# A bank split moved from token 334 to token 332, and GpSimd's low parts written as two operations

## The chip, the cores and the metric

The kernel runs on one core of a Trainium2 chip. The metric is the device time of one execution in microseconds (us); of several runs the median is shown. TensorE is called PE here (its matmuls PE, its weight loads PEld), VectorE DVE, ScalarE ACT, GpSimd POOL, and the DMA-issuing SyncE SP.

## The reference

One step of a small streaming encoder with two layers, on 528 prompt tokens (16 of them learned) and 8 sequences of 16 tokens that continue from carried state. All of it is float32.

```python
def trunk(x, ...):
    for i in range(DEPTH):                      # DEPTH = 2
        h = rmsnorm(x, norm_mix[i])
        if i % 2 == 0: m, s = gla_mixer(h, ...)         # gated linear attention
        else:          m, s = shortconv_mixer(h, ...)
        x = x + m
        f, s = conv_ffn(rmsnorm(x, norm_ffn[i]), ...)
        x = x + f
    return rmsnorm(x, norm_final), ...

def shortconv_mixer(h, buf, w_in, conv_w, w_out):
    bg, cg, u = jnp.split(h @ w_in, 3, axis=-1)
    y, new_buf = causal_dwconv(cg * u, buf, conv_w)     # depthwise, width 3, over tokens
    return (bg * y) @ w_out, new_buf

def conv_ffn(h, buf, w_up, conv_w, conv_b, w_down):     # 1024 -> 2 * 2816 -> 1024
    z = h @ w_up
    zc, new_buf = causal_dwconv(z, buf, conv_w)
    gate, up = jnp.split(zc + conv_b, 2, axis=-1)
    return (jax.nn.silu(gate) * up) @ w_down, new_buf
```

## The kernel before

The activations lie as x[128, 8, 656]: 1024 features in 8 tiles of 128 partitions, and for each tile a row of 656 tokens (528 prompt tokens, then 128 sample tokens), 4 bytes each, so that token t of a tile stands at byte 4t of the tile's row.

**Products.** Each float32 product is made of three passes in a 4-byte matmul type (fp32r): a high part (xh, wh, gh) and a low part (xl, wl, gl), as wh with xh, wh with xl, and wl with xh. The weights come in 512 KB units [128, 8, 128] into a ring of four. For every unit SP loads `raw`, ACT casts the high part `wh` (function `high`, line 1244), POOL subtracts to get the low part `wl` (function `low`, line 355; a few units are done by DVE at line 807), and only then may PE use the unit. A core's PSUM is used as four slots of two banks. A product's token range doesn't fit one bank of 512, so every pass is a **pair** of matmuls, one per bank, cut at a token that `banks(first, cut)` gives.

**Token ranges.** The products don't need the earliest tokens of the later stages, so a stage begins at token `first` and ends at 656: 0 in the attention's input projections, 8 in its output projection, 8 and 12 in the up projections of the ffn of layers 0 and 1 (`FIRST_Z`), 12 in the short convolution mixer (`FIRST_MIX`) and in the down projection of layer 0, 16 in the down projection of layer 1. The cut is `middle(first)`, half way, except in the up projections, where it is half way through the prompt part (`middle(first, PROMPT)`), so that DVE can take the prompt part of both banks in one operation.

**Stages.** PE's stream of work: attention projections (`project`, line 409, one unit = 8 feature tiles x 3 passes = 24 pairs), attention (to about 330 us), its output projection, then per layer the ffn in 11 groups: four up units (`z`), then `project_down` (line 425: 8 output tiles m, each two weight tiles x 3 passes = 6 pairs), with the mixer of layer 1 between the two ffns. The groups of an ffn run in a loop written for all engines. The order of work on each engine is written out by hand. For every output tile m of a down projection DVE adds the product to x (`add_to_x`, line 801) and with it frees the PSUM slot; PE waits for the slot (`open_slot`) four steps later. A `z` unit is taken by DVE in `take_padded` (lines 1032 to 1040) which frees its slot, then convolved (`convolve`, lines 1009 and 1013, three operations), and every second one gated (`gate_hidden`, lines 1020 to 1026). DVE reaches the adds of a down projection only behind the take and the convolution of the group's last `z` unit. The sum of squares for a norm is added by DVE at line 770 and summed over partitions by PE at line 437.

Of the kernel before, what the change touches and what calls it, by code (L numbers as in the profile page):

```python
# [21 lines left out]
F32 = mybir.dt.float32  # L22
# [141 lines left out]
def build(nc, x_in, w_in, wgd_in, wgu_in, par_in, reset_in, mask_in, s0_in, zc_in,  # L164
# [126 lines left out]

    def banks(first, cut):

        return (0, first, cut), (BANK, cut, TOK)
# [19 lines left out]
    def from_token(first, ap, p):  # L314

        return two(ap[:, first:TOK]), slot(p, (TOK - first) // 2)
# [27 lines left out]
    def _(pool):  # L344
# [8 lines left out]
        def low(j, done):  # L353
            pool.wait_ge(sem["hi_done"], done)
            pool.tensor_tensor(wl[:, j, :, :], raw[:, j, :, :], wh[:, j, :, :].bitcast(F32),  # L355
                               ALU.subtract).then_inc(sem["lo_done"], 1)
# [26 lines left out]
    def _(pe):  # L383
# [32 lines left out]
        def project_down(step, first, f0, n_ready, rings, i=0, release=1, g_count=None):  # L416
# [3 lines left out]
            for m in range(KT):  # L420
                p = open_slot(step(m), i)
                for f in range(2):
                    for w, v in ((wh, gh), (wh, gl), (wl, gh)):
                        for c, a, z in banks(first, middle(first)):
                            mm = pe.matmul(ps[:, p, c:c + z - a], w[:, rings[f], m, :], v[:, f0 + f, a:z],  # L425
                                           start=(f == 0 and w is wh and v is gh), stop=(f == 1 and w is wl))
                            if m == 0 and f == 0 and w is wh and v is gh and c:
                                mm.then_inc(sem["units_used"], release)
# [227 lines left out]
        for layer in range(2):  # L656
            if layer == 1:

                for g in range(MIX_G):
                    for j in range(6):  # L660
                        project(("mix", g, j), xh, xl, n_unit + 1, n_unit % RING, FIRST_MIX, middle(FIRST_MIX),
# [12 lines left out]
            def z_units(g, i=0, release=1, norm=None):  # L674
                nonlocal n_unit
                for j in range(4):
                    u = n_unit + j
                    project(("z", layer, g, j), xh, xl, 12 * i + (u + 1), u % RING, FIRST_Z[layer],
                            middle(FIRST_Z[layer], PROMPT), i=i,
# [68 lines left out]
    def _(dve):  # L748
# [49 lines left out]
        def add_to_x(p, m, first):  # L798

            tile, product = from_token(first, x[:, m, :], p)  # L800
            dve.tensor_tensor(tile, product, tile, ALU.add).then_inc(freed[p], 1)  # L801
# [241 lines left out]
        def z_unit(step, layer, z, j, i=0):  # L1043
# [5 lines left out]
            take_padded(p, j, rstd, FIRST_Z[layer], middle(FIRST_Z[layer], PROMPT))  # L1049
# [34 lines left out]
        def mixer():  # L1084
            dve.wait_ge(sem["zl_saved"], ZT)
            for g in range(MIX_G + 1):
                if g < MIX_G:
                    for e in range(2):
# [3 lines left out]
                        out, product = from_token(FIRST_MIX, bg[:, e, :], p)  # L1092
                        dve.tensor_tensor(out, product, two(rstd[:, FIRST_MIX:]), ALU.mult).then_inc(freed[p], 1)
                        p = take(("mix", g, 3 * e + 1))
                        out, product = from_token(FIRST_MIX, cg, p)
                        dve.tensor_tensor(out, product, two(rstd[:, FIRST_MIX:]), ALU.mult).then_inc(freed[p], 1)
# [6 lines left out]
                        take_padded(p, e, cg, FIRST_MIX, middle(FIRST_MIX))  # L1103
# [528 lines left out]
```

## Time and profile before

| | us |
|---|---|
| three runs | 1556.33, 1556.71, 1563.7 |
| median of them | 1556.71 |
| the profiled execution | 1557.0 |
| its span in the trace | 1555.2 |
| PE busy | 1532.7 (99%) |
| DVE busy | 1106.0 (71%) |
| POOL busy | 488.5 (31%) |
| ACT busy | 441.4 (28%) |

The time of an execution is its span plus 1.8 us around it. Matmuls overlap in the trace, so the mean time of one is longer than the pace at which they follow each other; the pace is read from the start times, or from the chain, where a run of matmuls stands with its length and its count. TensorE's granted clock was 2.4 GHz over all of the stretch from 330 to 1533 us.

### The profile page before, as it was taken

Reading aid. Unit: us, or ns where it says so; the run is one execution under the profiler, and the core shown is the slowest. Engines: PE = TensorE matmul, PEld = TensorE weight load, DVE = VectorE, ACT = ScalarE, POOL = GpSimd, SP = SyncE. Lnnn points to the kernel's source line nnn. Section 1 sums busy time; section 2 is a strip of 40 time slices with the busy share of each in tenths; the row PEclk is TensorE's granted clock in tenths of the full one; section 3 lists DMA queues with packets and bytes.
Section 4 is the critical chain, followed back from the end, with each engine's and each line's share of the span. In section 5 each row is a group of like instructions: output and inputs, shape, how many; then the busy total and the mean of one; then the engine's idle time right before and its main releaser. Section 6 shows DMA issues by size and latency. Waiting matters only on the chain.

```text
span 1555.2 us, 25977 instructions
## 1 busy us (share of the span) xinstructions
PE 1532.7 (99%) x10294; PEld 1514.5 (97%) x10294; DVE 1106.0 (71%) x1315; ACT 441.4 (28%) x692; POOL 488.5 (31%) x207
## 2 busy tenths in 40 slices
PE   7999999999999999999999999999999999999997
PEld 6999998899999999999999999999999999999996
DVE  6566665754977777777778645548977787777777
ACT  5355554343212121211215111115221212212123
POOL 2422221143233333323332333332333333233330
PEclk9999999999999999999999999999999999999998
DMA  6211116222222222122222222222222222222212
GB/s 216 80 55 55 55 55 239 90 72 69 68 76 74 68 81 79 57 80 71 78 71 65 92 82 68 82 68 78 66 78 72 77 81 66 68 81 67 77 47 78
DMA packets 34841, 123.76 MB, mean 80 GB/s; under 512 B 3888, under 2 KB 6832, under 8 KB 33616
## 3 DMA queue, kind: packets, MB, share of 16 engines
q1 hardware_dynamic: 31840, 108.37, 22.3%
q10 hardware_dynamic: 2928, 14.35, 2.5%
q8 instruction: 54, 0.88, 0.2%
q14 instruction: 19, 0.16, 0.0%
HBM read 114.48 MB, written 8.22 MB: 79 GB/s over the span
## 4 chain that ended last, share of the span: by engine, by line
PE 94%; DVE 3%; ACT 1%; DMA 1%; DVEq 1%; issue 0%; POOL 0%; SPq 0%; ACTq 0%
PE ps L409 64%; PE ps L425 21%; PE ps L611 2%; PE ps L511 2%; PE ps L710 1%; PE ps L635 1%; PE ps L563 1%; PE ps L525 0%; DVE sq L770 0%; DMA s<-states 0%; DMA raw<-w_units 0%; DVE x L1161 0%; PE ps L645 0%; DVE snew L979 0%; PE ps L492 0%; PE ps L437 0%
## 5 line engine op out<-in xcount | busy, mean ns | idle before, releaser
L355 POOL TENSOR_TENSOR wl<-raw,wh 128x1024 fp32r<-128x1024 f32 x190 | 472.3, 2492 | 966.9 <-ACT wh L1244 927.7
L409 PE MATMUL ps<-xh,wh 128*128 128x260 f32 (+3 forms) x2144 | 494.9, 312 | 0.0
L409 PE MATMUL ps<-xl,wh 128*128 128x260 f32 (+3 forms) x2144 | 493.5, 312 | 0.0
L409 PE MATMUL ps<-xh,wl 128*128 128x260 f32 (+3 forms) x2144 | 493.4, 312 | 0.0
L409 PEld LDWEIGHTS ps<-xl,wh 128*128 128x128 f32 x2144 | 382.5, 189 | 0.0
L409 PEld LDWEIGHTS ps<-xh,wh 128*128 128x128 f32 x2144 | 381.8, 189 | 0.7
L409 PEld LDWEIGHTS ps<-xh,wl 128*128 128x128 f32 x2144 | 382.2, 189 | 0.0
L1244 ACT ACTIVATE wh<-raw 128x1024 fp32r<-128x1024 f32 x196 | 204.2, 1055 | 302.1 <-PE ps L409 276.9
L801 DVE TENSOR_TENSOR x<-ps,x 128x644 f32<-128x644 f32 (+2 forms) x200 | 158.8, 823 | 94.7 <-PE ps L425 67.7
L1013 DVE SCALAR_TENSOR_TENSOR y<-zp,par,y 128x660 f32<-128x660 f32 (+1 forms) x192 | 185.7, 967 | 26.5 <-issue 21.7
L425 PE MATMUL ps<-gl,wh 128*128 128x322 f32 (+1 forms) x768 | 177.2, 312 | 0.0
L1389 ACT COPY zl<-zp 128x18 f32 (+1 forms) x88 | 18.3, 208 | 558.3 <-DVE y L1013 558.3
L425 PE MATMUL ps<-gh,wh 128*128 128x322 f32 (+1 forms) x768 | 175.9, 310 | 0.1
L425 PE MATMUL ps<-gh,wl 128*128 128x322 f32 (+1 forms) x768 | 175.2, 309 | 0.0
L425 PEld LDWEIGHTS ps<-gh,wh 128*128 128x128 f32 x768 | 129.7, 189 | 0.8 <-DVE x L801 0.7
L425 PEld LDWEIGHTS ps<-gh,wl 128*128 128x128 f32 x768 | 130.0, 189 | 0.0
L425 PEld LDWEIGHTS ps<-gl,wh 128*128 128x128 f32 x768 | 129.5, 189 | 0.0
L1009 DVE TENSOR_SCALAR y<-zp,par 128x660 f32<-128x660 f32 (+1 forms) x96 | 100.5, 1047 | 29.9 <-issue 27.0
L1032 DVE TENSOR_TENSOR zp<-ps,rstd 128x520 f32<-128x520 f32 (+1 forms) x88 | 61.1, 694 | 72.1 <-PE ps L409 68.7
L1026 DVE TENSOR_TENSOR gl<-hh,gh 128x644 fp32r<-128x644 f32 (+1 forms) x52 | 100.0, 1923 | 3.9
L1024 DVE CAST gh<-hh 128x644 fp32r<-128x644 f32 (+1 forms) x52 | 66.6, 1281 | 3.8
L1021 DVE TENSOR_TENSOR hh<-sg,y 128x128 f32<-128x128 f32 x44 | 52.2, 1187 | 0.0
(158 smaller groups left out, 1238.6 us busy)
## 6 DMA issues: line engine op xcount, KB each, us to landing
raw<-w_units SPq DMA_DIRECT2D x196, 512.0 KB, 3.5
s<-states ACTq DMA_DIRECT2D x4, 1024.0 KB, 6.0
state_sample<-snew ACTq DMA_DIRECT2D x4, 1024.0 KB, 4.1
x<-x_t SPq DMA_DIRECT2D x8, 328.0 KB, 8.3
x<-x_t ACTq DMA_DIRECT2D x1, 2624.0 KB, 13.1
y_t<-x SPq DMA_DIRECT2D x4, 384.0 KB, 2.4
y_t<-x SPq DMA_DIRECT2D x4, 256.0 KB, 2.2
ffn_last<-zl ACTq DMA_DIRECT2D x2, 396.0 KB, 3.4
```

What stands on the lines that cost most here:

```text
L355: pool.tensor_tensor(wl[:, j, :, :], raw[:, j, :, :], wh[:, j, :, :].bitcast(F32), ALU.subtract).then_inc(sem["lo_done"], 1)
L409: mm = pe.matmul(ps[:, p, c:c + z - a], w[:, ring, k, :], v[:, k, a:z], start=(k == 0 and w is wh and v is hi), stop=(k == KT - 1 and w is ...
L425: mm = pe.matmul(ps[:, p, c:c + z - a], w[:, rings[f], m, :], v[:, f0 + f, a:z], start=(f == 0 and w is wh and v is gh), stop=(f == 1 and ...
L511: return pe.matmul(queries(ps[:, p, :], a, z), ks[:, a:a + P], queries(qs, a, z), start=True, stop=True)
L801: dve.tensor_tensor(tile, product, tile, ALU.add).then_inc(freed[p], 1)
L1009: dve.tensor_scalar(out, src[:, first:YN], w_col(0), w_col(3) if bias else None, ALU.mult, ALU.add if bias else ALU.bypass)
L1013: last = dve.scalar_tensor_tensor(out=out, in0=src[:, first + j:YN + j], scalar=w_col(j), in1=out, op0=ALU.mult, op1=ALU.add)
L1021: dve.tensor_tensor(blocks(hh[:, PROMPT:TOK], SLEN), gate[1], blocks(up[:, SB:PADDED], SW)[:, :, 0:SLEN], ALU.mult)
L1024: dve.tensor_copy(gh[:, f, first:TOK], hh[:, first:TOK])
L1026: dve.tensor_tensor(gl[:, f, first:TOK], hh[:, first:TOK], gh[:, f, first:TOK].bitcast(F32), ALU.subtract).then_inc(sem["g_done"], 1)
L1032: dve.tensor_tensor(two(zp[:, zi, 2 + first:SB]), slot(p, cut - first), two(factor[:, first:PROMPT]), ALU.mult)
L1244: act.activation(wh[:, j, :, :], raw[:, j, :, :], ACT.Copy).then_inc(sem["hi_done"], 1)
```

## The change

`cut_of(first)` is `middle(first)` rounded down to a multiple of 4. It replaces `middle` in the down projections and the mixer's projections, and in the up projections of layer 1 it replaces the middle of the prompt part. Only ranges that begin at token 12 change: the mixer's and the down projection's pair goes from 322 and 322 tokens (cut at 334) to 320 and 324 (cut at 332), and layer 1's up pair from 258 and 386 (cut at 270) to 320 and 324. Ranges that begin at 0, 8 and 16 keep their cuts. `from_token` now gives a list, of one piece where both banks hold the same number of tokens, and of two where they don't: DVE's adds to x after a 12-token start, and its two takes per mixer tile, become two operations each; `take_padded` in layer 1 takes its other branch, three operations in place of two. And POOL's `low` becomes two operations over half of the feature tiles each, of which the second signals.

```diff
+    def cut_of(first):
+        return (first + (TOK - first) // 2) // 4 * 4
...
     def from_token(first, ap, p):
-        return two(ap[:, first:TOK]), slot(p, (TOK - first) // 2)
+        cut = cut_of(first)
+        if 2 * cut == first + TOK:
+            return [(two(ap[:, first:TOK]), slot(p, cut - first))]
+        return [(ap[:, a:z], ps[:, p, c:c + z - a]) for c, a, z in banks(first, cut)]
+
+    Z_CUT = (middle(FIRST_Z[0], PROMPT), cut_of(FIRST_Z[1]))
...
         def low(j, done):
             pool.wait_ge(sem["hi_done"], done)
-            pool.tensor_tensor(wl[:, j, :, :], raw[:, j, :, :], wh[:, j, :, :].bitcast(F32),
-                               ALU.subtract).then_inc(sem["lo_done"], 1)
+            for ks in (slice(0, KT // 2), slice(KT // 2, KT)):
+                last = pool.tensor_tensor(wl[:, j, ks, :], raw[:, j, ks, :], wh[:, j, ks, :].bitcast(F32),
+                                          ALU.subtract)
+            last.then_inc(sem["lo_done"], 1)
...
-                        for c, a, z in banks(first, middle(first)):
+                        for c, a, z in banks(first, cut_of(first)):
...
-                        project(("mix", g, j), xh, xl, n_unit + 1, n_unit % RING, FIRST_MIX, middle(FIRST_MIX),
+                        project(("mix", g, j), xh, xl, n_unit + 1, n_unit % RING, FIRST_MIX, cut_of(FIRST_MIX),
...
-                            middle(FIRST_Z[layer], PROMPT), i=i,
+                            Z_CUT[layer], i=i,
...
         def add_to_x(p, m, first):
-            tile, product = from_token(first, x[:, m, :], p)
-            dve.tensor_tensor(tile, product, tile, ALU.add).then_inc(freed[p], 1)
+            for tile, product in from_token(first, x[:, m, :], p):
+                last = dve.tensor_tensor(tile, product, tile, ALU.add)
+            last.then_inc(freed[p], 1)
...
-            take_padded(p, j, rstd, FIRST_Z[layer], middle(FIRST_Z[layer], PROMPT))
+            take_padded(p, j, rstd, FIRST_Z[layer], Z_CUT[layer])
```

The mixer's two takes (`bg`, `cg`) change in the same way as `add_to_x`, and its `take_padded` gets `cut_of(FIRST_MIX)`.

The instructions on PE at the start of layer 1's ffn, where the mixer's last down projection ends and the first up unit begins; before:

```order
L425 MATMUL ps<-gh,wh 128x322 x2
L425 MATMUL ps<-gl,wh 128x322 x2
L425 MATMUL ps<-gh,wl 128x322 x2
L409 MATMUL ps<-xh,wh 128x258
L409 MATMUL ps<-xh,wh 128x386
L409 MATMUL ps<-xl,wh 128x258
L409 MATMUL ps<-xl,wh 128x386
```

and in the changed program, at the same place:

```order
L436 MATMUL ps<-gh,wh 128x320
L436 MATMUL ps<-gh,wh 128x324
L436 MATMUL ps<-gl,wh 128x320
L436 MATMUL ps<-gl,wh 128x324
L436 MATMUL ps<-gh,wl 128x320
L436 MATMUL ps<-gh,wl 128x324
L420 MATMUL ps<-xh,wh 128x320
L420 MATMUL ps<-xh,wh 128x324
```

The number of matmuls and their order stay; a pair has 644 tokens before and now.

On DVE, in layer 1's ffn, a `z` unit is taken, convolved and gated; before:

```order
L1032 TENSOR_TENSOR zp<-ps,rstd 128x516
L1040 TENSOR_TENSOR zp<-ps,rstd 128x8x16
L1009 TENSOR_SCALAR y<-zp,par 128x656
L1013 SCALAR_TENSOR_TENSOR y<-zp,par,y 128x656 x2
L1020 TENSOR_TENSOR hh<-sg,y 128x512
```

and now:

```order
L1047 TENSOR_TENSOR zp<-ps,rstd 128x320
L1049 TENSOR_TENSOR zp<-ps,rstd 128x196
L1052 TENSOR_TENSOR zp<-ps,rstd 128x8x16
L1021 TENSOR_SCALAR y<-zp,par 128x656
L1025 SCALAR_TENSOR_TENSOR y<-zp,par,y 128x656 x2
L1032 TENSOR_TENSOR hh<-sg,y 128x512
```

One operation on the 516 prompt tokens has become two, ahead of the convolution; the rest is as before. In layer 0's down projections DVE's `x<-ps,x 128x644` has become `128x320` and `128x324` in the same way.

## Rows read from the trace of the kernel before

**Rows 1.** The page, part 1: busy times, share of the span, instructions.

```profile
PE 1532.7 (99%) x10294; PEld 1514.5 (97%) x10294; DVE 1106.0 (71%) x1315; ACT 441.4 (28%) x692; POOL 488.5 (31%) x207
```

**Rows 2.** Busy times by stretch (length, busy us and counts, granted clock).

```profile
330.00:1533.00 1203.00, 1202.87 (x8069) 1201.21 (x8068) 877.09 (x996) 276.04 (x472) 400.62 (x164) 1.00 0.24 73
```

**Rows 3.** Groups of PE's matmuls by form: count | busy us, mean ns | idle.

```profile
L409 PE MATMUL ps<-xh,wl 128*128 128x386 f32 x352 | 120.5, 342 | 0.0
...
L409 PE MATMUL ps<-xh,wl 128*128 128x388 f32 x352 | 119.6, 340 | 0.0
...
L425 PE MATMUL ps<-gh,wl 128*128 128x322 f32 x480 | 109.7, 310 | 0.0
...
L409 PE MATMUL ps<-xh,wl 128*128 128x322 f32 x384 | 88.1, 311 | 0.0
```

**Rows 4.** The chain in order of time: start us, us, what, matmuls.

```profile
441.29 28.53 PE ps L409 x192
...
555.57 14.31 PE ps L425 x96
...
943.24 42.81 PE ps L409 x288
...
1130.09 14.04 PE ps L425 x96
1144.13 28.60 PE ps L409 x192
1172.73 7.03 PE ps L425 x48
...
1258.30 14.07 PE ps L425 x96
```

**Rows 5.** PE's timeline, output projection: first and last of 44 rows (a row: one pair).

```profile
333.12 0.46 PE L409 MATMUL ps<-oh,wh 128*128 128x324 f32 x2
...
345.83 0.46 PE L409 MATMUL ps<-ol,wh 128*128 128x324 f32 x2
```

**Rows 6.** Timelines of DVE, POOL and PE around the first norm.

```profile
21.23 5.82 DVE L770 TENSOR_TENSOR sq<-sq 128x656 f32<-128x656 f32 x2
...
20.90 5.44 POOL L355 TENSOR_TENSOR wl<-raw,wh 128x1024 fp32r<-128x1024 f32 x2 [18.19 <-ACT wh L1244]
...
27.10 1.37 PE L437 MATMUL ps<-sq,ones 128*128 128x328 f32 x4 [0.98 <-DVE sq L770]
```

**Rows 7.** Timeline at 1172 us: DVE and POOL behind a group's last z unit.

```profile
1172.76 0.70 DVE L1032 TENSOR_TENSOR zp<-ps,rstd 128x516 f32<-128x516 f32 x1 [0.78 <-PE ps L409]
...
1173.38 0.28 DVE L1040 TENSOR_TENSOR zp<-ps,rstd 128x128 f32<-128x128 f32 x1
1174.05 2.81 DVE L1009 TENSOR_SCALAR y<-zp,par 128x656 f32<-128x656 f32 x1 [0.39 <-issue]
1174.10 2.40 POOL L355 TENSOR_TENSOR wl<-raw,wh 128x1024 fp32r<-128x1024 f32 x1 [6.76 <-ACT wh L1244]
...
1178.91 2.28 DVE L801 TENSOR_TENSOR x<-ps,x 128x640 f32<-128x640 f32 x3
```

**Rows 8.** DVE's timeline: the first add to x of two other groups.

```profile
561.51 0.82 DVE L801 TENSOR_TENSOR x<-ps,x 128x644 f32<-128x644 f32 x1
...
1264.21 0.82 DVE L801 TENSOR_TENSOR x<-ps,x 128x640 f32<-128x640 f32 x1
```

**Rows 9.** POOL's two subtractions: duration ns min/median/max.

```profile
L355 POOL TENSOR_TENSOR wl<-raw,wh x190: 2357/2409/4182, 20.9 to 1519.5; 128x1024 fp32r<-128x1024 f32 x190
...
L367 POOL TENSOR_TENSOR ol<-qk,oh x8: 1571/1604/2180, 277.6 to 325.2; 128x656 fp32r<-128x656 f32 x8
```

**Rows 10.** DVE's timeline in the mixer: a take in three operations.

```profile
864.37 0.49 DVE L1035 TENSOR_TENSOR zp<-ps,cg 128x322 f32<-128x322 f32 x1 [2.58 <-PE ps L409]
864.78 0.35 DVE L1037 TENSOR_TENSOR zp<-ps,cg 128x194 f32<-128x194 f32 x1
865.04 0.28 DVE L1040 TENSOR_TENSOR zp<-ps,cg 128x128 f32<-128x128 f32 x1
```

More of the change, by code:

```diff
@@ L1091, in mixer @@
                         p = take(("mix", g, 3 * e))
-                        out, product = from_token(FIRST_MIX, bg[:, e, :], p)
-                        dve.tensor_tensor(out, product, two(rstd[:, FIRST_MIX:]), ALU.mult).then_inc(freed[p], 1)
+                        for (out, product), (factor, _) in zip(from_token(FIRST_MIX, bg[:, e, :], p),
+                                                               from_token(FIRST_MIX, rstd, p)):
+                            last = dve.tensor_tensor(out, product, factor, ALU.mult)
+                        last.then_inc(freed[p], 1)
                         p = take(("mix", g, 3 * e + 1))
-                        out, product = from_token(FIRST_MIX, cg, p)
-                        dve.tensor_tensor(out, product, two(rstd[:, FIRST_MIX:]), ALU.mult).then_inc(freed[p], 1)
+                        for (out, product), (factor, _) in zip(from_token(FIRST_MIX, cg, p),
+                                                               from_token(FIRST_MIX, rstd, p)):
+                            last = dve.tensor_tensor(out, product, factor, ALU.mult)
+                        last.then_inc(freed[p], 1)
                         dve.drain()
@@ L1102, in mixer @@
                             dve.wait_ge(sem["cl_saved"], E - 1)
-                        take_padded(p, e, cg, FIRST_MIX, middle(FIRST_MIX))
+                        take_padded(p, e, cg, FIRST_MIX, cut_of(FIRST_MIX))
                         dve.drain()
```

## Prediction

> **What bounds the kernel now.** I read the page first: PE is busy 99% of the span, DVE 71%, POOL 31% [rows 1]. Since overlapping matmuls make "busy" a weak word, I read the busy times by stretch next: between 330 and 1533 us PE stands still for 0.13 of 1203 us, at a granted clock of 1.00, which is 2.4 GHz [rows 2]. So three quarters of the time is the pace at which PE's matmuls follow each other, and nothing else. An operation removed from DVE or POOL there is worth nothing unless PE was waiting for it; a faster pair of matmuls is worth all of its gain.
>
> Then I read that pace from the chain, as length over pairs (two matmuls make a pair) [rows 4]:
> - layer 1 down, 320 and 320 tokens: 14.04 / 48 = 292.5 ns
> - layer 0 down, 322 and 322: 14.31 / 48 = 298.1 ns
> - mixer, 322 and 322: 42.81 / 144 = 297.3 ns
> - layer 1 up, 258 and 386: 28.60 / 96 = 297.9 ns
> - layer 0 up, 260 and 388: 28.53 / 96 = 297.2 ns
>
> and for the output projection, 324 and 324, from the first and last start of 44 pairs: 12.71 / 43 = 295.6 ns [rows 5]. The reader is to see that 644 tokens cost as much as 648 or more, while 640 cost 5 ns less: layer 1's up pair has four tokens fewer than layer 0's and is 0.7 ns slower. By form the same shows: 386 columns have a mean of 342 ns, 388 columns 340 [rows 3]. What the slow pairs share is their cut: 334 or 270, not a multiple of 4. A token is 4 bytes, so I count groups of four tokens (16 bytes) that a piece touches. Cut at 334, both pieces touch the group 332 to 335: 81 + 81 = 162 groups for 161 groups' worth of tokens. At 270 it is 65 + 97 = 162. The aligned 648 is 162 too, and 640 is 160. The pace follows the groups.
>
> **The change, part by part.**
>
> *The cut at 332.* The new pair touches 80 + 81 = 161 groups. Its price is not in the trace. From halves: a 320 piece is 146.3 ns, a 324 piece is between 147.8 (rows 5) and 148.6 (half of layer 0's up pair, rows 4); together 294.1 to 294.9, and I take 294.5 [rows 4, 5]. How many pairs: a form's count stands for one of three passes and one of two equal pieces, so 386 columns make 352 x 3 = 1056 pairs, the mixer's 322 make 384 x 3 / 2 = 576, and the down projections' 322 make 480 x 3 / 2 = 720 [rows 3]. The sum:
> - up, layer 1: 1056 x (297.9 - 294.5) = 3.6 us
> - mixer: 576 x (297.3 - 294.5) = 1.6 us
> - down at 12 tokens: 720 x (298.1 - 294.5) = 2.6 us
>
> Together 7.8 us; at 294.9 it is 6.8, at 294.1 it is 8.7.
>
> What speaks against it is a rule: the Trainium skill, page "TensorE: Matmul & The Clock Gate", section "Back-to-back issue gap", gives a gap of N/2.4 + 2.5 ns for N columns, in which only the number of columns counts. By that rule a pair of 644 costs 273.3 ns before and after, and this part would save 0; the rows stand 25 ns above it and don't grow with N as it says between 644 and 648. The same skill, page "SBUF — State Buffer", section "Specifications (TRN2)", states 16-byte cachelines with a penalty for each new line; with that the rows agree.
>
> *DVE's extra operations.* An add to x or a take that was one operation becomes two: 120 adds (15 down projections of 8), 16 takes in the mixer, 44 in layer 1's up units, 180 in all. The price of one more: a take of 516 tokens holds DVE 0.62 us (1172.76 to 1173.38), while 322 and 194 tokens hold it 0.67 (864.37 to 865.04) [rows 7, 10]. That is 0.05 to 0.06 us each, 11 us of DVE in all. It lies beside PE's work: DVE is idle 29% of the time. It is on a path at one place per group, below.
>
> *POOL's two halves, first norm.* POOL's subtraction and a DVE operation with two inputs in SBUF shut each other out here: two adds of squares on 656 tokens take 5.82 us together while POOL does two subtractions from 20.90 on, where a 640-token add takes 0.82 [rows 6, 7]. Each waits out one whole POOL operation, and PE then stands still 0.98 us for the sum [rows 6]. Price of a half: POOL takes 2357 ns for 1024 elements and 1571 for 656, so 2.14 ns an element and 0.17 us fixed; 512 elements make 1.26 us [rows 9]. The two DVE adds then wait for one half each, about 1.2 us less each, and the sum is there 2 us earlier. PE's 0.98 us go. Nothing else held PE there, so the gain is 1.0 us.
>
> *POOL's two halves, in the groups.* Behind the last up unit of each group, DVE must take it, convolve it (three operations), and then make the first add to x, since PE's fifth output tile needs that slot. At 1172 us PE comes to the slot at 1172.73 + 7.03 = 1179.76 [rows 4] and the add ends at 1179.73 [rows 7], so no time is left over. In two other groups the add ends at 562.33 and 1265.03 [rows 8], where PE wants the slot at 555.57 + 14.31/2 = 562.73 and 1258.30 + 14.07/2 = 1265.34 [rows 4]: 0.4 and 0.3 us spare. There are 20 such places. In this path DVE's line 1009 waits out POOL: it ends at 1176.86, 0.36 us after POOL's 1176.50 [rows 7]. With halves of 1.26 us it ends at 1174.10 + 1.26 + 0.36 = 1175.72; but the second half then takes the port to 1176.98, and the next operation (line 1013, two inputs in SBUF) waits for that and ends some 0.7 us later, 1177.7 in place of about 1177.9. So cutting POOL's operation in two does not free this path: 0.2 us better, less 0.06 for the extra take or add. I book 0 for the 18 places with spare time. At the two places where a gate stands between the second and third add (812 and 1043 us in the program's order) two or three adds are longer and PE comes earlier: 0.3 us lost together.
>
> *POOL itself.* 190 x 0.17 = 32 us more work; it idles 69% of the span, PE is never seen waiting for it between 330 and 1533 us [rows 1, 2]. Nothing.
>
> **Sum:** 7.8 + 1.0 - 0.3 = 8.5 us off the profiled execution's 1557.0, which is 0.3 above the median of the runs shown: **1548.5 us**, 0.53% under the median.
>
> **The rivals.**
>
> *Only the column count matters.* Then 644 tokens stay at their pace and 1.0 - 0.3 us remain: 1556.3 us. For it: a stream of columns is the plain picture, and 2 columns more or less are near the scatter. Against it: the pace of 258 and 386, from 96 pairs in a row, over that of 260 and 388. Chance 0.10. The skill's rule of columns above would give this.
>
> *The path behind a group eats a part.* If a POOL half costs what 656 elements cost, 1.57 us [rows 9], line 1009 ends at 1176.03, the second half at 1177.6, and the first line 1013 at 1178.3: 0.35 later, 0.41 with the extra operation. With 0.3 us spare that is 0.1 at some 17 places and 0.4 at three: 3 us, 1551.5 us. For it: the fixed cost of a POOL operation is a line through two points, and no half was ever seen. Chance 0.17.
>
> *Slower.* The same path at a higher price. To be slower than before by 0.5% (7.8 us), 16.3 us must be lost, 0.82 at each of 20 places beyond 0.3 spare; the path gets 0.2 longer for each 0.1 of a half, so a half would have to cost 1.93 us, more than 656 elements. At 2.0 us: 1.27 longer, 0.97 lost at each, 19 us, 1567.5 us. Chance 0.04.
>
> **How the numbers follow.** My forecast has 0.69. Its own range is 6.8 to 8.7 for the cut, plus 0.5 us either way for the places behind the groups: 1547 to 1550. The whole range reaches down to 1546.3, for a pace at the low bound and all waits at the groups gone, and up to 1554, which takes in the path rival and leaves out the column rival and the slower one (0.14) and a little below. A measurement can tell about 0.5% from no change, 7.8 us, so the border lies at 1548.9. The forecast stands just beyond it: of its 0.69 I give 0.46 to faster and 0.23 to no change; the path and column rivals are no change. Faster 0.48 (0.02 for gains not seen), same 0.48, slower 0.04.
>
> **What the changed profile would show.** The chain's runs: layer 1 up 28.27 us for 192 matmuls in place of 28.60, layer 0 down 14.14 in place of 14.31, the mixer's 288 matmuls 42.4 in place of 42.81; if these stand still, the grouping by four is wrong. Layer 0 up (28.53) and layer 1 down (14.04) must not move. PE's wait for `sq` at 27 us is gone. POOL's operation has a median near 1.26 us, twice as many; a median near 1.6 speaks for the path rival, and then gaps stand after the fourth output tile of the down projections. What would make me wrong most: a new pair at 296 ns or more, or one that also pays for unequal pieces.

## The result, and the profile after

| | before | after | ratio, interval |
|---|---|---|---|
| median of 6 runs each | 1557.65 | 1545.71 (1543.26 to 1549.83) | 0.9915, 0.9888 to 0.9942 |
| the same again: 23 and 6 runs | 1556.92 | 1547.22 (1545.14 to 1554.17) | 0.9941, 0.992 to 0.9962 |
| profiled execution | 1557.0 | 1546.99 | |
| its span | 1555.2 | 1545.2 | |

The ratios are estimated from the single runs and differ a little from the quotients of the medians (0.9923 and 0.9938). The change made the kernel faster by 0.6 to 0.85%, 10.0 us in the pair of profiled executions. The first measurement's median lies 0.6 us below the low end of the range that was given (1546.3), the second inside it. Against the profiled pair the forecast was 1.5 us short: 8.5 us said, 10.0 found. Its main cause, the pace of the pairs, was right; two of its terms were not, as the section behind the experiments works out.

The page of the changed kernel, part 1, which answers to [rows 1]:

```profile
PE 1523.1 (99%) x10294; PEld 1505.0 (97%) x10294; DVE 1028.9 (67%) x1495; ACT 441.1 (29%) x692; POOL 562.3 (36%) x397
```

DVE has 180 operations more and is busy 77 us less. What an operation of DVE spends blocked by POOL counts as its busy time, so this is the first sign that the halves did more than the forecast granted them.

Its busy times over the stretch that answers to [rows 2] (length, PE, PEld, DVE, ACT, POOL busy with counts, granted clock):

```profile
330.00:1522.00 1192.00, 1192.00 (x8059) 1190.72 (x8058) 802.64 (x1174) 275.98 (x472) 463.72 (x328) 1.00 0.23 73
```

PE stands still for nothing at all now (0.13 us before), at the same clock of 2.4 GHz. That 0.13 us understates what PE lost before: an idle time in the trace ends at a start, but begins at a modelled end, and the experiments below find 0.7 us that PE wins back there with POOL's halves alone. The rest is pace. The chain in order of time, as in [rows 4]:

```profile
440.39 28.54 PE ps L420 x192
...
554.29 14.13 PE ps L436 x96
...
938.66 42.38 PE ps L420 x288
...
1123.25 14.03 PE ps L436 x96
1137.28 28.23 PE ps L420 x192
...
1250.07 14.04 PE ps L436 x96
...
1503.73 19.82 PE ps L721 x120
```

The three lengths that should shorten did: layer 0's down projection 14.31 to 14.13 us (14.14 said), the mixer 42.81 to 42.38 (42.4 said), layer 1's up units 28.60 to 28.23 (28.27 said). The two that should stand still did: 28.53 to 28.54, and 14.04. One by one, from the start times of complete pairs:

| pair, tokens | before, ns | after, ns |
|---|---|---|
| layer 1 up, 258/386 to 320/324 | 297.86 | 294.16 |
| mixer, 322/322 to 320/324 | 297.97 | 294.16 |
| down, 322/322 to 320/324 | 298.55 | 294.51 |
| down, 320/320 | 292.8 | 292.43 |
| layer 0 up, 260/388 | 297.21 | 297.16 |

POOL's operation, duration ns min/median/max, which answers to [rows 9]:

```profile
L365 POOL TENSOR_TENSOR wl<-raw,wh x380: 1262/1303/3077, 21.2 to 1510.1; 128x512 fp32r<-128x512 f32 x190
```

Close to the 1260 that the forecast had. The first norm, timelines of DVE, POOL and PE, as in [rows 6]:

```profile
21.52 3.61 DVE L781 TENSOR_TENSOR sq<-sq 128x656 f32<-128x656 f32 x2
25.06 1.31 DVE L849 CAST wgd<-wgd_raw 128x128 fp32r<-128x128 f32 x1
26.44 1.21 DVE L851 TENSOR_TENSOR wgd<-wgd_raw,wgd 128x128 fp32r<-128x128 f32 x1
...
21.20 6.30 POOL L365 TENSOR_TENSOR wl<-raw,wh 128x512 fp32r<-128x512 f32 x4 [18.48 <-ACT wh L1260]
...
25.87 1.27 PE L448 MATMUL ps<-sq,ones 128*128 128x328 f32 x4
27.70 0.49 PE L503 MATMUL ps<-xh,wgd 128*32 128x328 f32 x2 [0.56 <-DVE wgd L851]
```

The two adds of squares take 3.61 us instead of 5.82, and PE's wait for `sq` is gone. But behind them the cast and the subtraction on 128x128, which make the low part of the gate's weights, hold DVE 1.31 and 1.21 us beside POOL's later halves (0.21 and 0.29 us before), and PE now waits 0.56 us for that. So part of the 1.0 us that the forecast booked here did not come. How much is not sharp: behind the gate's weights PE begins the next projection at 32.52 us, 33.11 before, but at 32.05 in another execution of the changed kernel and at 31.53 with the halves alone, since the first matmul of the program starts at 7.6 to 9.4 us. Up to the second norm's sum, which PE reaches at 378.59 us and at 379.30 before, it is 0.7 us; that stretch holds the attention with its scatter.

### The profile page after: what moved, and what is told of

The parts are those of the page before. It is cut to its first block, busy times and chain, and to the rows that moved or that the text cites. A ratio compares the mean times of both kernels' runs of the same rounds, so it can differ in the third digit from the quotient of the medians.

```text
span 1545.2 us, 26347 instructions
## 1 busy us (share of the span) xinstructions
PE 1523.1 (99%) x10294; PEld 1505.0 (97%) x10294; DVE 1028.9 (67%) x1495; ACT 441.1 (29%) x692; POOL 562.3 (36%) x397
## 4 chain that ended last, share of the span: by engine, by line
PE 96%; DVE 2%; ACT 1%; DVEq 1%; DMA 0%; POOL 0%; issue 0%; SPq 0%; ACTq 0%
PE ps L420 64%; PE ps L436 22%; PE ps L522 2%; PE ps L622 2%; PE ps L721 1%; PE ps L574 1%; PE ps L646 1%; PE ps L536 1%; DMA raw<-w_units 0%; DVE x L1177 0%; PE ps L656 0%; PE ps L503 0%; ACT xh L1214 0%; PE ps L493 0%; DVE sq L781 0%; DVEq L976 0%
## 5 line engine op out<-in xcount | busy, mean ns | idle before, releaser
L365 POOL TENSOR_TENSOR wl<-raw,wh 128x512 fp32r<-128x512 f32 x380 | 546.0, 1461 | 883.6 <-ACT wh L1260 846.9
L420 PE MATMUL ps<-xh,wh 128*128 128x320 f32 (+2 forms) x2144 | 494.5, 312 | 0.0
L420 PE MATMUL ps<-xl,wh 128*128 128x320 f32 (+2 forms) x2144 | 491.3, 310 | 0.0
L420 PE MATMUL ps<-xh,wl 128*128 128x320 f32 (+2 forms) x2144 | 490.8, 310 | 0.0
L812 DVE TENSOR_TENSOR x<-ps,x 128x320 f32<-128x320 f32 (+2 forms) x320 | 167.5, 569 | 107.0 <-PE ps L436 78.1
L436 PE MATMUL ps<-gh,wh 128*128 128x320 f32 (+1 forms) x768 | 175.6, 310 | 0.0
L436 PE MATMUL ps<-gh,wl 128*128 128x320 f32 (+1 forms) x768 | 175.1, 309 | 0.0
L436 PE MATMUL ps<-gl,wh 128*128 128x320 f32 (+1 forms) x768 | 174.8, 309 | 0.0
L1021 DVE TENSOR_SCALAR y<-zp,par 128x660 f32<-128x660 f32 (+1 forms) x96 | 71.8, 748 | 29.8 <-issue 26.9
L1044 DVE TENSOR_TENSOR zp<-ps,rstd 128x520 f32<-128x520 f32 x44 | 30.6, 696 | 58.6 <-PE ps L420 58.5
```

The lines of the kernel that those rows point to most:

```text
L365: last = pool.tensor_tensor(wl[:, j, ks, :], raw[:, j, ks, :], wh[:, j, ks, :].bitcast(F32), ALU.subtract)
L420: mm = pe.matmul(ps[:, p, c:c + z - a], w[:, ring, k, :], v[:, k, a:z], start=(k == 0 and w is wh and v is hi), stop=(k == KT - 1 and w is ...
L812: last = dve.tensor_tensor(tile, product, tile, ALU.add)
L1021: dve.tensor_scalar(out, src[:, first:YN], w_col(0), w_col(3) if bias else None, ALU.mult, ALU.add if bias else ALU.bypass)
L1044: dve.tensor_tensor(two(zp[:, zi, 2 + first:SB]), slot(p, cut - first), two(factor[:, first:PROMPT]), ALU.mult)
```

## The experiments

Timed runs of this kernel scatter by several microseconds for a reason that lies in the attention (last section), so most readings below are of one stretch of the trace without that reason: from the first matmul of the second norm's sum to the first matmul of the last down projection, 1135 us of PE's work in the kernel before, all of it up, mixer and down units but for three norms' sums. Two executions of the changed kernel agree in it to 0.01 us. "Layer 1" is the part of it from the norm ahead of layer 1's ffn on.

| kernel | stretch, us | of it layer 1 |
|---|---|---|
| before | 1134.77 | 431.69 |
| after | 1124.98 | 427.48 |
| after, again | 1124.99 | 427.49 |
| cut alone | 1130.76 | 431.22 |
| halves alone | 1134.03 | 431.30 |
| cut, one POOL unit in six in halves (d1) | 1127.01 | 427.48 |
| cut, another one in six (z0) | 1127.43 | 428.05 |
| after, gh and gl 8 bytes off | 1132.59 | |
| after, 4 bytes off | 1133.83 | |
| after, 16 bytes off | 1126.37 | |
| after, cut at 330 | 1132.20 | |
| after, cut at 336 | 1126.32 | |
| after, POOL in quarters | 1124.93 | |
| after, two more edits (even_hold) | 1124.41 | |

### The changed kernel again, and its two parts alone

`after_again` is the changed kernel itself. `cut_only` has the cut and POOL's whole operation:

```diff
-            for ks in (slice(0, KT // 2), slice(KT // 2, KT)):
-                last = pool.tensor_tensor(wl[:, j, ks, :], raw[:, j, ks, :], wh[:, j, ks, :].bitcast(F32),
-                                          ALU.subtract)
-            last.then_inc(sem["lo_done"], 1)
+            pool.tensor_tensor(wl[:, j, :, :], raw[:, j, :, :], wh[:, j, :, :].bitcast(F32),
+                               ALU.subtract).then_inc(sem["lo_done"], 1)
```

`halves_only` is the kernel before with the minus lines in place of the plus lines.

> The changed kernel once more, for its time beside the kernel before on one chip. If the 10.0 us between the two profiled spans is the change and the rest of the 11.9 us between the medians is scatter, the ratio comes out near 0.9935 (10 us less). If something works in the timed runs that the profiled pair doesn't show, it stays at 0.9915 or below.

> The cut at 332 with GpSimd's low part in one operation. Cut theory: the new pairs run at 294.2 to 294.5 ns whatever GpSimd does, so this alone gives 8.6 us (1056 pairs x 3.7 ns + 576 x 3.1 + 720 x 3.9) less whatever the places behind the groups cost now that the takes and adds are longer: I expect 8 us, ratio 0.995, and TensorE waits of 0.1 to 0.3 us at several groups. Wait theory: the two halves carry a good part of the gain (2 us or more), so the cut alone gives 6.5 us or less.

> GpSimd's halves with the cuts of before. Cut theory: pairs stay at 297.2 to 298.5 ns, the wait before the first norm shrinks by 0.6 us, those at 823 and 1179 us (0.5 us together) go: 1.2 us faster, ratio 0.9992. Wait theory: 3 us or more.

Measured: after again 1547.22 us, ratio 0.9941 (0.992 to 0.9962), so the first of the two readings in its expectation: the change is about the 10 us of the profiled pair, and the rest of the first 11.9 us is scatter. The cut alone 1553.45, ratio 0.9986 (0.9968 to 1.0004). The halves alone 1556.04, ratio 0.9994 (0.9975 to 1.0012). Neither part alone can be told from no change, both together are 9.7 us. In the stretch: the halves give 0.7 us, the cut 4.0, both 9.8. So the halves are worth 5.8 us once the cut is there. The forecast, which had them at next to nothing in the groups, missed this, and so did the expectation for the cut alone: its up and mixer pairs are as fast as the changed kernel's (294.16 ns), and yet it gains only 4 us of the cut's 9. All of the 5.8 us between it and the changed kernel lies in the down projections: 2.1 us in layer 0's and 3.7 in layer 1's, where one takes 14.4 to 14.5 us in place of 14.04. PE's waits in the kernel with the cut alone:

```profile
PE ps L434 <- DVE x L810: 1.2, 6, 0.4
```

and PE's timeline at one of the places, behind layer 1's last up unit of a group:

```profile
1257.54 0.45 PE L434 MATMUL ps<-gh,wl 128*128 128x320 f32 x2
1258.15 0.56 PE L434 MATMUL ps<-gh,wh 128*128 128x320 f32 x2 [0.16 <-DVE x L810]
```

From 1257.54 to 1258.15 it is 0.61 us where a pair takes 0.29: 0.3 us lost at the fifth output tile, for the slot that the first add to x frees. It is the place that the forecast named. The view of waits shows 0.16 of the 0.3 us here, and 1.2 us of some 5 in all, since it counts only idle time, and a matmul's modelled end covers the rest.

### Which POOL operation does it

The diff is that of `half_d1`; `half_z0` has (4, 10) in place of (3, 9). Both have the cut, with POOL's operation whole except for one unit in six, in layer 1's ffn alone. `half_d1` halves the operation that runs while DVE gates the group's second pair of units, `half_z0` the next one, which runs while DVE takes and convolves the last up unit:

```diff
-        def low(j, done):
+        def low(j, done, halves=False):
...
-            for ks in (slice(0, KT // 2), slice(KT // 2, KT)):
+            parts = (slice(0, KT // 2), slice(KT // 2, KT)) if halves else (slice(0, KT),)
+            for ks in parts:
...
+                        low(o % RING, 12 * i + (done + o + 1), o in (3, 9))
```

> The kernel with the cut alone, and in layer 1's ffn GpSimd's low part in halves for one unit in six: the group's second down unit, whose operation falls on VectorE's gl (the gate ahead of the last two up units). Read from layer 1's stretch, from the norm sum to the first last-down matmul, 431.2 us with the cut alone and 427.5 with all in halves. Upstream theory: VectorE's delay at that gate makes its convolution, ScalarE's next cast and so GpSimd's next operation late, and puts that one onto the convolution behind the group's last up unit; with this half the path to the first add to x gets 0.5 us or more shorter than with the cut alone and TensorE's waits go: 427.5 to 428.5 us. Place theory (what my prediction worked out, GpSimd's start taken as given): only the operation that falls on the convolution counts, so this changes nothing: 431.

> The kernel with the cut alone, and in layer 1's ffn halves for another unit in six: the next group's first up unit, whose operation falls on VectorE's convolution (line 1019 there) behind the group's last up unit. Place theory: 0.2 us at each of 9 places, the stretch takes 429.4 us. Upstream theory: GpSimd still starts late, the second half falls on the next operation of the convolution, and little is won: 429.5 to 431 us, the first add to x at 7.0 to 7.2 us behind TensorE's start of the down projection.

Measured, single executions: 1552.94 and 1554.58 us. In layer 1's part of the stretch the cut alone takes 431.22 us, `half_d1` 427.48, which is all that the changed kernel has, and `half_z0` 428.05. Outside layer 1, where nothing was halved, both stay within 0.2 us of the cut alone. So one step earlier, a half brings all of it, as the upstream theory had it. On the operation that falls on the convolution it brings 3.2 of the 3.7 us, more than either theory gave it (429.4 and 429.5 to 431): the first add to x ends 0.3 us earlier, against PE's start, than with the cut alone, near the 0.2 us that the prediction worked out for such a half, and since the path was 0.2 to 0.3 us too long, that is nearly enough. There the second half does fall on the convolution's second operation (1.68 us in place of 0.90), as the prediction said:

```profile
1258.58 2.80 POOL L366 TENSOR_TENSOR wl<-raw,wh 128x512 fp32r<-128x512 f32 x2 [6.82 <-ACT wh L1267]
...
1260.40 1.68 DVE L1032 SCALAR_TENSOR_TENSOR y<-zp,par,y 128x656 f32<-128x656 f32 x1 [0.17 <-issue]
```

How the half one step earlier works is to be seen in the timelines of POOL and DVE. The cut alone:

```profile
1252.48 2.38 POOL L364 TENSOR_TENSOR wl<-raw,wh 128x1024 fp32r<-128x1024 f32 x1 [6.83 <-ACT wh L1258]
...
1251.02 0.49 DVE L1045 TENSOR_TENSOR zp<-ps,rstd 128x320 f32<-128x320 f32 x1 [0.67 <-PE ps L418]
...
1252.47 2.75 DVE L1019 TENSOR_SCALAR y<-zp,par 128x656 f32<-128x656 f32 x1 [0.50 <-issue]
...
1257.28 1.55 DVE L810 TENSOR_TENSOR x<-ps,x 128x640 f32<-128x640 f32 x2
```

The changed kernel, the same group:

```profile
1249.93 2.54 POOL L365 TENSOR_TENSOR wl<-raw,wh 128x512 fp32r<-128x512 f32 x2 [4.99 <-ACT wh L1260]
...
1250.11 0.49 DVE L1047 TENSOR_TENSOR zp<-ps,rstd 128x320 f32<-128x320 f32 x1 [2.29 <-PE ps L420]
...
1251.56 1.27 DVE L1021 TENSOR_SCALAR y<-zp,par 128x656 f32<-128x656 f32 x1 [0.50 <-issue]
...
1254.89 1.55 DVE L812 TENSOR_TENSOR x<-ps,x 128x640 f32<-128x640 f32 x2
```

And what comes ahead of it, the product that ends the gating (`gl`) beside POOL's operation on the unit before; in the kernel before:

```profile
1250.47 2.87 DVE L1026 TENSOR_TENSOR gl<-hh,gh 128x640 fp32r<-128x640 f32 x1
...
1250.13 2.52 POOL L355 TENSOR_TENSOR wl<-raw,wh 128x1024 fp32r<-128x1024 f32 x1 [3.99 <-ACT wh L1244]
```

and in `half_d1`:

```profile
1247.82 3.14 POOL L366 TENSOR_TENSOR wl<-raw,wh 128x512 fp32r<-128x512 f32 x2 [3.99 <-ACT wh L1267]
...
1248.04 1.77 DVE L1045 TENSOR_TENSOR gl<-hh,gh 128x640 fp32r<-128x640 f32 x1
```

The reader is to see two things. First, a DVE operation with two inputs in SBUF that starts just behind POOL's waits out all of it: `gl` takes 2.87 us beside a whole operation, 1.77 beside a half, and 0.82 where POOL does nothing. The Trainium skill, page "SBUF — State Buffer", section "Who interferes with whom", says that the shared port pair is held for the whole instruction and that the order of issue decides who blocks; by that rule, the trace agrees.

Second, `gl` being 1.1 us earlier moves everything behind it: DVE's convolution, ACT's gate and its next cast, and with the cast POOL's next operation. Counted from PE's first matmul of the down projection, ACT's cast starts at 0.5 us with the cut alone and at -0.6 in `half_d1`, and POOL's operation at 1.7 and 0.55. In the changed kernel that operation starts at 1249.93, ahead of the take (1250.11). It is not over when the convolution begins: its second half holds the first operation of it for 1.27 us, where that operation takes 0.62 undisturbed, and the later ones are free. In the cut alone it starts at 1252.48, 1.5 us behind the take, and the convolution's first operation, from 1252.47, waits out all of it (2.75 us).

In layer 1's groups the first add to x ends, after PE's first matmul of the down projection, at 6.7 to 6.9 us before (7.2 in the first group), 7.2 to 7.3 with the cut alone, 6.9 to 7.0 in `half_z0`, 6.1 to 6.2 in `half_d1`, and 5.7 to 5.9 after; PE wants the slot at 7.0.

The kernel with the halves alone shows the same at the old cut. There POOL's operation starts 1.5 to 1.6 us earlier against PE's start than before, and the first add ends at 5.3 to 5.6 us (5.8 in the first group), 1.4 us earlier than before where the prediction had 0.2. One such group, in which PE's first matmul starts at 1255.34 us (in the same group of the kernel before it starts at 1258.14, and the first add at 1264.21):

```profile
1255.09 2.54 POOL L356 TENSOR_TENSOR wl<-raw,wh 128x512 fp32r<-128x512 f32 x2 [4.92 <-ACT wh L1246]
...
1260.04 2.28 DVE L803 TENSOR_TENSOR x<-ps,x 128x640 f32<-128x640 f32 x3
```

Why the cut alone is worse here than no cut: PE's four up units became 0.37 us shorter (28.60 to 28.23), and the work of DVE, ACT and POOL behind them did not. The same group's POOL operation stands 1.3 us behind PE's first matmul of the down projection before and 1.7 in the cut alone, 0.4 later, and the add that waits it out ends 0.4 later too (6.9 and 7.3). That fits, and was not tested by itself.

### What a pair's pace hangs on

The forecast counted the groups of four tokens (16 bytes) that a piece touches. To part this from the alignment of the piece's **start**, `gh_shift` moves the products' inputs gh and gl by 2 tokens (8 bytes) in SBUF, with the changed kernel's pieces unchanged; `gh_shift4` by 1 token, `gh_shift16` by 4:

```diff
-    gh = sb("gh", [P, 4, TOK], F32R)
-    gl = sb("gl", [P, 4, TOK], F32R)
-    assert at[0] <= sr_at
-    at[0] = sr_at
+    gh_wide = sb("gh", [P, 4 * TOK + 2], F32R, offset=qk_at)
+    gl_wide = sb("gl", [P, 4 * TOK + 2], F32R, offset=qk_at + 4 * T4 + 32)
+    gh, gl = (t[:, 2:2 + 4 * TOK].rearrange("p (f t) -> p f t", f=4) for t in (gh_wide, gl_wide))
+    at[0] = sr_at + 64
```

The edits move more than these inputs: gl lies a further 32 bytes on, and every tile behind them (y, sg and the rest) 64 bytes. Both are multiples of 16.

And two other cuts, by two lines in `cut_of` (`cut_336` returns 336):

```diff
+        if first == 12:
+            return 330
```

> The changed kernel with the hidden activations gh and gl moved by two tokens (8 bytes) in SBUF, so that every piece read by a down projection begins and ends in the middle of a group of four tokens (16 bytes), its lengths unchanged. Nothing is left out. Groups theory: pieces of 320 touch 81 groups and pieces of 324 touch 82, so layer 1's down pair goes from 162 ns groups-wise 160 to 162, from 292.4 to 295 to 298 ns, and the 320/324 pair from 294.5 to 298 or more; up projections stay at 294.2. Length theory (only whether a piece's length is a multiple of four counts): nothing moves.

> The changed kernel with gh and gl moved by one token (4 bytes). If any start off 16 bytes costs the same, the pairs are at 298.8 and 301.1 ns as with a move by two tokens. If a piece pays by how much of a group it splits off, or 8 bytes count as well, they are higher by 1 ns or more.

> The changed kernel with gh and gl moved by four tokens (16 bytes). If the boundary that counts is 16 bytes, the down projections' pairs are back at 292.4 and 294.5 ns. If it is 32 or 64 bytes, the pieces that began at token 16 and 336 (multiples of 64 bytes) now don't, and the 320/320 pair stays above 294.

> The changed kernel with the cut at token 330 for ranges that begin at 12: 318 and 326 tokens, the second piece beginning 8 bytes behind a boundary of 16. VectorE's and GpSimd's operations are as in the changed kernel. Start theory (a piece that begins off 16 bytes costs 3.3 ns or more): pairs at 297.5 to 298 ns in up and mixer, 298.5 in down, 8.6 us more than the changed kernel between the second norm sum and the last down projection (1133.6 against 1125.0). Rival (the two sizes must be multiples of four, wherever they begin) says the same; both die if the pairs stay at 294.2.

> The changed kernel with the cut at token 336: 324 and 320 tokens, both beginning on 16 bytes. If 332 is special in no other way, pairs at 294.2 and 294.5 ns and the same stretch, 1125.0 us.

Measured, single executions: 1560.17, 1559.05, 1554.93, 1550.91 and 1553.98 us; the stretches stand in the table. The chain, 96 matmuls (48 pairs) of a down projection, layer 0 (320/324) and layer 1 (320/320). With 8 bytes:

```profile
603.14 14.51 PE ps L436 x96
...
1133.05 14.34 PE ps L436 x96
```

with 4 bytes:

```profile
601.74 14.46 PE ps L436 x96
...
1132.19 14.40 PE ps L436 x96
```

with 16 bytes:

```profile
603.11 14.14 PE ps L436 x96
...
1130.02 14.13 PE ps L436 x96
...
1172.40 14.03 PE ps L436 x96
```

The changed kernel has 14.13 and 14.03. By complete pairs, ns:

| pair | unshifted | 16 bytes | 8 bytes | 4 bytes |
|---|---|---|---|---|
| down, 320/324 | 294.51 | 295.54 | 301.12 | 302.20 |
| down, 320/320 | 292.43 | 293.43 | 298.79 | 300.10 |

One group and four tokens more cost 2.1 ns (292.43 to 294.51). Shifted by 8 bytes a pair touches two groups more, which by the count is 4.2 ns; it pays 6.4 to 6.6. By 4 bytes it touches as many groups as by 8, and pays 7.7. So the count of groups is not the price. In these runs a piece that **begins** off a 16-byte boundary pays 3.2 to 3.3 ns at 8 bytes off and 3.8 at 4 bytes off, for 320 and for 324 tokens. About 1.0 ns of a pair's rise comes with the 16-byte shift too, where the expectation had none; against that column the price is 2.7 to 2.8 and 3.3. This 1.0 ns is a mean of two kinds of group: in layer 1 every second down projection takes 14.03 us, as unshifted, and the others 14.13, which is 2.1 ns a pair. So there is a second effect besides the 16 bytes. It differs between the groups of one loop, and what it is stays open.

The other cuts agree on the boundary, and not on one price. Cut at 330, the second piece begins 8 bytes off; cut at 336 it begins on a boundary. The chain with 330:

```profile
636.68 14.22 PE ps L438 x96
...
937.39 42.87 PE ps L422 x288
```

and with 336:

```profile
602.91 14.16 PE ps L438 x96
...
944.30 42.24 PE ps L422 x288
...
1000.63 42.56 PE ps L422 x288
...
1143.36 28.38 PE ps L422 x192
```

The mixer's first 288 matmuls take 42.87 us at 330, as at 334 before (42.81), and 42.24 at 336, as at 332 (42.38); its next 288 take 42.56 at 336. By complete pairs, mixer and layer 1 up together, it is 297.6 ns at 330. At 336 the mixer has 294.0 ns, and layer 1's up pair 295.6 where 294.2 was expected: 28.38 us for 192 matmuls in place of 28.23. This is why the stretch at 336 is 1126.32 us, 1.3 longer than the 1125.0 expected, though every piece begins on 16 bytes; the cause was not found. The down projection at 330 has 296.72 ns, so its unaligned start costs 2.2 ns where 334 cost 4.0, and the stretch is 1132.20 us where 1133.6 was expected; why stays open. Taken over all of these runs, an unaligned start costs between 2 and 4 ns. The Trainium skill, page "SBUF — State Buffer", section "Specifications (TRN2)", has 16-byte cachelines and a penalty for each cross to a new line; by that rule an unaligned start costs a line, and the runs agree on the boundary, but it has no price, and 4 bytes off costs more than 8, which the count of lines doesn't give.

### What is left: quarters, layer 0's up pair, and the first norm

`quarters` makes POOL's operation four of two feature tiles each:

```diff
-            for ks in (slice(0, KT // 2), slice(KT // 2, KT)):
+            for ks in (slice(0, 2), slice(2, 4), slice(4, 6), slice(6, 8)):
```

`even_hold` gives layer 0's up units an even pair (324/324 in place of 260/388) and lets POOL's first two units wait for the sum of squares:

```diff
-    Z_CUT = (middle(FIRST_Z[0], PROMPT), cut_of(FIRST_Z[1]))
+    Z_CUT = (cut_of(FIRST_Z[0]), cut_of(FIRST_Z[1]))
...
+        pool.wait_ge(sem["sum_done"], 1)
```

> The changed kernel with GpSimd's low part in four operations. By the line through the lengths seen (512 elements 1.29 us, 1024 2.39) a quarter takes 0.74 us and the unit 2.95. VectorE's waits get shorter still, but TensorE waits for it nowhere between 330 us and the last down projection, so that stretch stays at 1125.0 us; only the wait before 28 us can shrink, by 0.5 us. If something else in that stretch still hung on VectorE, it would get shorter than 1124.5.

> The changed kernel with two more edits: layer 0's up projections are cut at token 332 too (324 and 324 in place of 260 and 388), and GpSimd begins its first two low parts only when VectorE has added the last square of the first norm. From the traces so far a 324/324 pair runs at 295.6 ns and a 260/388 pair at 297.2, so 1056 pairs give 1.7 us, and TensorE's wait for the gate's weights before 28 us shrinks by 0.5 us. Ratio to the kernel before 0.9925 to 0.993. The rival is that a pair's two sizes don't matter and the 1.6 ns are the output projection's own: then 0.5 us alone, read from layer 0's up runs, 28.53 us for 192 matmuls in place of 28.38.

Measured: quarters 1551.58 us in a single execution, stretch 1124.93, so nothing beyond the halves. POOL's group there (count | busy us, mean ns), and, from PE's waits (us in all, times, longest), one that it did not have before:

```profile
L365 POOL TENSOR_TENSOR wl<-raw,wh 128x256 fp32r<-128x256 f32 x760 | 617.6, 845 | 812.0 <-ACT wh L1260 777.1 <-DVE wl L819 34.2
```

```profile
PE ps L721 <- POOL wl L365: 0.6, 1, 0.6
```

Once PE waits for nothing in the stretch, shorter locks are worth nothing, and POOL's own unit gets longer until PE waits for it at the last down projection.

`even_hold`: 1547.65 us, ratio 0.9931 (0.9905 to 0.9957) to the kernel before. The layer 0 up pair went from 297.16 to 296.93 ns only, chain:

```profile
614.81 28.38 PE ps L421 x192
...
657.17 28.63 PE ps L421 x192
```

28.38 and 28.63 us beside 28.54, and so through the whole layer, group by group in turn: by complete pairs 295.6 and 298.2 ns. In every second group the even pair is as fast as the expectation had it, and in the others it is slower than 260/388, so that on the whole the two are level. It is again an effect that hangs on the group and not on how the piece is aligned, and its cause was not found. The hold did what it should: PE's waits for `sq` and for the gate's weights are both gone, and the two adds of squares take 1.76 us. The stretch is 0.6 us shorter than the changed kernel's, and the first projection behind the gate's weights starts at 31.83 us (32.52 and 32.05 in the two executions of the changed kernel). The timed runs can't tell it from the changed kernel.

## Why the prediction came close, and which of its steps failed

The kind of gain was right, and two steps of the sum were not. The largest term, the cut, was sized at 7.8 us and measured 9.0. And the places behind the groups, booked at 0.3 us lost, gave 0.8 us, because the step "cutting POOL's operation in two does not free this path" is wrong. The sum, by its own terms, in the two profiled executions:

| term | predicted, us | measured, us |
|---|---|---|
| cut: layer 1 up, 1056 pairs | 3.6 | 3.9 |
| cut: mixer, 576 pairs | 1.6 | 2.2 |
| cut: down at 12 tokens, 720 pairs | 2.6 | 2.9 |
| first norm, with all up to the second norm's sum | 1.0 | 0.7 |
| places behind the groups (what is left of the stretch) | -0.3 | 0.8 |
| tail | 0 | -0.5 |
| sum | 8.5 | 10.0 |

The median of the first six runs is a further 1.9 us lower than this pair gives; the second set, at 9.7 us between the medians, doesn't have them, and scatter of that size stands in the last section.

- **What bounds the kernel, right.** All of the gain of the cut is pace, and PE stands still no more than before.
- **The cut, right in place and sign, 1.2 us short: the term that was mis-sized.** The old pairs of the mixer and the down projections were read from one run of the chain each (297.3 and 298.1 ns), as if every run had the same pace. They don't: the mixer's first 504 matmuls go at 298.8 ns a pair and every second down projection at 299.0, as these lines of the kernel before show, and over all complete pairs it is 297.97 and 298.55. The new pair is 294.16 to 294.51 where 294.5 was taken. This term came out just outside its own bounds (6.8 to 8.7), at 9.0: 1056 x 3.70 + 576 x 3.81 + 720 x 4.04 ns.

```profile
598.42 14.35 PE ps L425 x96
...
853.59 75.30 PE ps L409 x504
```

- **Why it is so, half right.** The boundary of four tokens, 16 bytes, is what counts. But the number of groups touched doesn't give the times of the shifted inputs, and the start of a piece off the boundary does, though at a price that varies from 2 to 4 ns. Both theories say that 332 is faster than 334. That the wrong one gave nearly the right number is luck.
- **POOL's halves in the groups: the step whose mechanism failed.** The prediction put it so: "cutting POOL's operation in two does not free this path". It worked through one POOL operation, at the start time that it had in the trace. That start is itself the end of a path through DVE's `gl`, which waited out the POOL operation before. Where the start stays (`half_z0`), its arithmetic is near: 0.3 us where it had 0.2. With every operation halved, the one on the path starts earlier against PE, at 0.0 us behind PE's first down matmul in place of 1.3 in the group shown, and holds the convolution's first operation 1.27 us in place of 2.53. The first add to x came 1.0 to 1.3 us earlier in layer 1 (1.4 with the halves alone), not 0.2, and the places that were booked at -0.3 us gave 0.8, which are waits of the old kernel that are gone.
- **The path rival, right in mechanism, wrong in what sets it off.** Its price of a half (1.57 us) did not come, 1.30 did. But the path is the narrow place that it was said to be: with the cut alone and whole operations it eats 5 us of 9. The forecast had 0.3 us spare at these places and did not see that a faster PE spends it: each group's up units in layer 1 got 0.37 us shorter, the path behind them did not. That the sum still came near is in part luck: a loss of 5 us that it didn't see was undone by a gain of 5.8 us that it didn't see either.
- **The first norm, some tenths of a us short.** "Nothing else held PE there" was wrong: the gate's low weights were next, behind the same port.
- **The tail, missed.** From the last down projection to the end of the span it is 41.47 us in the chain, 40.97 before. The two pieces that differ are the down projection's 120 matmuls, 19.82 us in place of 19.68, and the last norm's second pair, which falls behind the clock's step down to 1.2 GHz at 1535.9 us and takes 0.79 us; before, the step came at 1546.7 us, as that pair ended, and it took 0.45:

```profile
1535.96 0.79 PE ps L752 x2
```

```profile
1546.34 0.45 PE ps L741 x2
```

Together they are 0.48 us. I have no experiment on it.

- **The column-count rival is dead**: 644 tokens in both, and 3.7 to 4.0 ns between them. The rule of the Trainium skill that the prediction sets beside it (page "TensorE: Matmul & The Clock Gate", section "Back-to-back issue gap") is stated there for a single matmul in isolation, which the prediction leaves out; this kernel's stream of matmuls doesn't follow it, with 146 ns for 320 columns where it gives 136. **The slower one** would have needed a half of 1.93 us.
- **DVE's extra operations**: nothing, as said. PE waits for none of the 180.

## What to carry to other kernels

Where PE is the bound and its moving operand has 4-byte elements, cut a token range so that every piece begins on 16 bytes, and then measure: of the aligned cuts tried here 332 was 1.3 us better than 336, and an uneven pair was on the whole no loss. When PE gets faster, look at every buffer that PE just finds free, since its spare time shrinks by what was gained. And when an operation is blocked by another engine's lock, ask what sets that engine's start as well: halving the operation *one step earlier* was worth all of the 3.7 us in layer 1.

## What the runs showed that was not expected

Executions of one program differ by up to 12 us, and in the profiled ones it lies in one place, the attention's state update between about 245 and 320 us. PE's granted clock there drops to 1.2 GHz for some stretches, others in each execution. Busy times over 230 to 330 us (PE, PEld, DVE, ACT, POOL, granted clock), of the changed kernel, of the same program again, and of the cut alone:

```profile
230.00:330.00 100.00, 98.85 (x623) 87.01 (x622) 63.20 (x103) 38.95 (x58) 19.37 (x12) 0.97 0.36 135
```

```profile
230.00:330.00 100.00, 99.88 (x568) 87.66 (x568) 61.80 (x101) 37.38 (x56) 16.19 (x10) 0.86 0.36 135
```

```profile
230.00:330.00 100.00, 98.25 (x641) 87.22 (x641) 64.79 (x105) 41.46 (x62) 19.06 (x10) 1.00 0.36 135
```

A mean of 0.97 is some 6 of 100 us at half clock, 0.86 is some 28. From the first norm's sum to the second's it takes 352.7, 360.8 and 349.2 us in these three, so 0.4 to 0.5 us are lost per microsecond at half clock. PE is busy 98 to 100% of that stretch in all three, so what it did ahead of a fall is not told apart by its busy share. The kernel before has 0.97 there too, like the changed one, so the profiled pair (10.0 us) is a fair comparison; this scatter may well be the 1.9 us that the first medians have beyond it. What makes the clock fall in one execution and not in another was not found.

The other one is the price of an unaligned start, 2 to 4 ns on a matmul of 146 to 149 ns, 2% or so, in a kernel where the matmuls of lines 420 and 436 are 86% of the chain.
